# Differential attention: GpSimd takes the difference of the second head's keys, VectorE keeps the first head's and the meta columns

## The chip, the core and the metric

The kernel runs on one core of a Trainium2 chip. It has five engines with their own instruction streams, which wait for each other only through semaphores: TensorE (matrix products, into PSUM), VectorE, ScalarE, GpSimd and SyncE (which here only issues DMAs; GpSimd issues some too). In the profile they are PE (and PEld, its weight loads), DVE, ACT, POOL and SP. The metric is the device time of one execution in microseconds (us); the kernel is launched once.

## What is computed

The reference is a chain of two transformer blocks on 512 tokens of width 1024. The first block has two layers and 16 meta tokens ahead of the sequence (528 positions). Each layer mixes four branches: a windowed attention with sinks (A), an attention with rotary positions (B), a differential attention (C) and a bidirectional gated linear attention (D). The change lies in C:

```
s = einsum(q, k) * scale + bias            # per head two components, comp 0 and 1
p = softmax(s)                             # over all 528 keys
a = p[:, 0] - lam * p[:, 1]                # the difference
o = einsum(a, v)
o = rms_norm(o, sub_g) * (1 - lambda_init)
```

## The kernel before

It is written directly in instructions of each engine, so each engine does its work in the order in which its function issues it. `att` is the list of attention steps. A step of C is one tile of 128 queries (the fifth tile has the 16 meta queries; layer 1 leaves it out) and one pair of heads. Its four cells are two heads with two components each, so layer 0 has 10 such steps and layer 1 has 8.

One step runs like this. TensorE makes the scores of the four cells (L1656; L1649 makes those of the meta keys). VectorE takes the meta scores to SBUF (L3331, L3339), then adds the bias and takes the row minimum, one instruction per cell (`minima`, L3315; 512 columns, and a short one that reads the minimum out). ScalarE does the exponentials with their sums (`exps`, L2519). VectorE takes the reciprocals (L3351) and, in L3354, the factor `cfac` = -lam * sum of comp 0 / sum of comp 1 of each head, and marks them with the semaphore `att_r`. Then `difference` (L3365) computes for each of the two heads p0 = p0 + cfac * p1 in place over 528 columns, 16 meta and 512 keys, with one scalar_tensor_tensor each, and marks `att_mix`. `kept` is where in the tile `temps` the four cells of a step lie: 4 x 528 columns, two steps in turn.

TensorE then transposes the differences (`turn_probs(c, 0)` for the meta columns of both heads, L1686, and the keys of the first head, L1689; `turn_probs(c, 1)` for those of the second, L1689); ScalarE copies them out of PSUM (L2533, L2536); TensorE multiplies by the values (L1715), and L1701 spreads the reciprocals. Each iteration n of TensorE's `attention` does the scores of step n, the values of step n - 2, the first transposition of step n - 1, then a `fill_piece` (24 matrix products of another branch, L1747 to L1749) and then the second transposition of step n - 1. VectorE's iteration n does `ratios` and `difference` of step n - 1 and then the minima of step n, and at some steps `scaled` (L3389) and a subtraction that splits weights (L2951).

GpSimd has no part in C before. Ahead of the attention of layer 0 it issues the first five of 24 sets of DMAs (`layer_step`, through `block_sums`, L1333 and L1335), which add up weights of layer 1 in DRAM; each set waits (`sums_moved`) until the one before has landed. In layer 1 it issues the last of these sets and three of another chain (`last_step`). It then waits for `rope`, its part of the rotary stage (L1198, L1216, L1219, L1223), which stands in the attention A that follows C. `head_roots`, `head_stats`, `head_ratios` and `head_spread` belong to the norms of C's and D's heads, later in each layer.

Of the kernel before, what the change touches and what calls it, by code (L numbers as in the profile page):

```python
# [278 lines left out]
def build(nc, ins, out_dram):  # L279
    with ExitStack() as ctx:  # L280
# [213 lines left out]
        def level_product(eng, e, src, rows, lev, upper):  # L494
# [29 lines left out]
        names += """att_scores att_meta att_min att_es att_exp att_esink  # L524
            att_r att_mix att_turned att_pt att_ptm att_pv att_spread att_out y_ready
            c_squared c_stat c_stat_ready c_rooted c_spread c_ready""".split()

        names += """sums_rounded log_high log_low gate_floored dz_gate dz_log state_cleared g_sums g_exp g_kf g_query_x g_key_x g_z g_ez
            g_kz g_pairs g_masked g_at g_half g_o g_state g_unit state_ready o_squared o_stat o_stat_ready o_rooted
            o_spread o_scaled dmix_ready""".split()  # L530

# [581 lines left out]
        def stat_blocks(kind, l):  # L1113

            return [(P, 0, 16), (META, 16, 20)][:1 if kind == "c" and l else 2]

        def planes(rows):

            return 1 + (NLEV - 1 if rows == P else 4)
# [27 lines left out]
        def _(pool):  # L1147
# [116 lines left out]
            def head_roots(kind, l):  # L1264

                for i, (rows, a, z) in enumerate(stat_blocks(kind, l)):
                    ap = ostat[0:rows, a:z]
                    pool.wait_ge(S[kind + "_stat_ready"], 2 * l + i + 1)
                    nc.gpsimd.tensor_tensor(ap, ap, neghalf[0:rows, :].to_broadcast([rows, z - a]), ALU.pow
                                            ).then_inc(S[kind + "_rooted"], 1)  # L1270

# [43 lines left out]
            def block_sums(step, wp, n):  # L1315
# [3 lines left out]
                for q in range(NSUMS):  # L1319
# [11 lines left out]
                    for out, x, plus in moves:  # L1331
# [5 lines left out]
                        moved_sums[0] += 16  # L1337

            for ly in layers:
                l = ly["l"]  # L1340
                if l:
                    full(pool, layers[l - 1]["ffn"]["down"][1][-1])
                    pool.wait_ge(S["ada_summed"], MODS // 2)
                    load_biases()
                for step in range(19, 24) if l else range(5):
                    layer_step(step)
                for step in range(3) if l else ():
                    last_step(step)
                rope(ly)
                for step in () if l else range(5, 9):  # L1350
                    layer_step(step)
                for step in range(3, 6) if l else ():
                    last_step(step)
                first_gate_lows(ly)
                head_roots("c", l)
                key_factors(ly)
                head_roots("o", l)
                residual_back(l)
                if l == 0:
                    ada_stream()  # L1360
                    residual_out(ly["ffn"]["ready"])
            else:
                second_block()
# [4 lines left out]
        def _(pe):  # L1368
# [293 lines left out]
            def turn_probs(c, j):  # L1662
                n, rows = c["n"], c["rows"]
                if c["kind"] == "C":
                    pe.wait_ge(S["att_mix"], c["mixed0"] + 2)
                else:
                    pe.wait_ge(S["att_exp"], c["cell0"] + (2 if c["metas"] else j + 1))
# [146 lines left out]
            def head_stats(kind, l, sq, tiles):  # L1814

                pe.wait_ge(S[kind + "_squared"], 2 * (l + 1))
                for t, (a, z) in tiles:
                    for hp in range(2):
                        last = mm(PS[0:z - a, 5, 4 * t + 2 * hp:4 * t + 2 * hp + 2], sq[hp][:, a:z], headmean,
                                  start=True, stop=True, skip_group_check=True)  # L1820
                last.then_inc(S[kind + "_stat"], 1)

            def head_spread(kind, l, tiles):

                pe.wait_ge(S[kind + "_rooted"], 2 * l + len(stat_blocks(kind, l)))
                for hp in range(2):
                    flat = PS[:, 2 * hp:2 * hp + 2, :].rearrange("p a b -> p (a b)")
                    for t, (a, z) in tiles:
                        for c0, c1 in [(a, z)] if z <= 512 else [(a, 512), (512, z)]:
                            for i in range(2):  # L1830
                                h = 4 * t + 2 * hp + i
                                last = mm(flat[64 * i:64 * i + 64, c0:c1], ostat[0:z - a, h:h + 1].to_broadcast([z - a, HD]),
                                          ident[0:z - a, c0 - a:c1 - a], start=True, stop=True, skip_group_check=True)
                last.then_inc(S[kind + "_spread"], 1)

# [1042 lines left out]
        def _(dve):  # L2878
# [480 lines left out]
            def difference(c):  # L3359
# [3 lines left out]
                for j in range(2):  # L3363
                    p0, p1 = (SB[0:rows, c["kept"] + 2 * j + comp, :] for comp in range(2))
                    V.scalar_tensor_tensor(out=p0, in0=p1, scalar=cfac[0:rows, 2 * (n % 4) + j:2 * (n % 4) + j + 1],  # L3365
                                           in1=p0, op0=ALU.mult, op1=ALU.add).then_inc(S["att_mix"], 1)
# [92 lines left out]
            def head_ratios(kind, l):  # L3459

                dve.wait_ge(S[kind + "_stat"], l + 1)
                for rows, a, z in stat_blocks(kind, l):
                    V.tensor_scalar(ostat[0:rows, a:z], PS[0:rows, 5, a:z], EPS, None, ALU.add
                                    ).then_inc(S[kind + "_stat_ready"], 1)

# [45 lines left out]
            def linear_attention(ly):  # L3511
# [67 lines left out]
                merge(ly, 1)  # L3579
                dve.wait_ge(S["c_spread"], l + 1)  # L3580
                c0 = META * l
# [34 lines left out]
                merge(ly, made[0] + 2)  # L3616
                dve.wait_ge(S["o_spread"], l + 1)
                dve.wait_ge(S["o_scaled"], 2 * (l + 1))
# [440 lines left out]
```

## Time and profile before

| | |
|---|---|
| time, median of 3 runs | 2983.24 us (2982.55 to 2983.50) |
| the profiled execution | 2986.24 us, its span 2984.4 us |
| TensorE busy | 2930.9 us, 98% |
| VectorE, ScalarE, GpSimd busy | 1909.2, 1138.4, 377.6 us |
| C in layer 0 | from about 99 to 172 us |
| C in layer 1 | from about 1152 to 1211 us |
| mean granted clock of TensorE | 0.993 |

Busy time of TensorE is modelled and is not its peak. "Idle before" in brackets is how long an engine had waited ahead of an instruction, and for whom. A VectorE instruction is recorded from its issue, and the next one is issued some 0.08 us before it ends. "x2" joins two instructions in a row.

### The profile page before, as it was taken

To read this page: it belongs to the slowest core of one execution; us is meant where nothing else is said; L and a number is where in the kernel's file an instruction comes from. 1 tells how busy PE (TensorE), PEld (TensorE's weight loads), DVE (VectorE), ACT (ScalarE), POOL (GpSimd) and SP (SyncE) were. 2 spreads that over 40 slices of the span, in tenths; PEclk is the share of its full clock that TensorE was granted. 3 is DMA by queue.
4 is the path that set the end of the run, shared out by engine and by line. 5 is a ranking of instruction groups with operands and counts; after the bars stand their busy time and mean duration, and the time that the engine had idled before them with its cause. 6 is when DMAs were issued, how large, how long until landed. Compare 5 with 4: busy or idle time off the path is not lost.

```text
span 2984.4 us, 57272 instructions
## 1 busy us (share of the span) xinstructions
PE 2930.9 (98%) x23772; PEld 2627.7 (88%) x23772; DVE 1909.2 (64%) x3760; ACT 1138.4 (38%) x2030; POOL 377.6 (13%) x610
## 2 busy tenths in 40 slices
PE   9999999999999999999999999999999999999998
PEld 8777999999999998789999899987888886799997
DVE  5574677557777756647765767677636555685565
ACT  4655223232212235552323434344222232664353
POOL 0242433000000020324320000001100000000000
PEclk9999999999999999999999999999999999999999
DMA  6725766234555574347533444438723331134452
GB/s 205 211 57 139 187 147 164 72 142 157 196 192 170 193 212 132 75 122 188 145 117 114 156 142 161 156 125 210 190 89 134 139 128 43 58 115 156 143 174 91
DMA packets 119513, 428.69 MB, mean 144 GB/s; under 512 B 14248, under 2 KB 16680, under 8 KB 114264
## 3 DMA queue, kind: packets, MB, share of 16 engines
q1 hardware_dynamic: 67032, 261.52, 25.5%
q0 software_dynamic: 52224, 163.51, 20.8%
q8 instruction: 190, 3.11, 0.4%
q14 instruction: 67, 0.55, 0.1%
HBM read 414.35 MB, written 109.01 MB: 175 GB/s over the span
## 4 chain that ended last, share of the span: by engine, by line
PE 88%; DVE 5%; ACT 4%; issue 2%; DMA 1%; POOL 1%; SPq 0%; DVEq 0%; ACTq 0%; POOLq 0%
PE acc L1385 14%; PE acc L1386 13%; PE acc L1387 13%; PE acc L1847 5%; PE acc L1848 5%; PE acc L1849 5%; PE acc L2113 4%; PE acc L2114 4%; PE acc L2115 4%; ACT temps L2519 2%; PE acc L1715 2%; PE acc L1656 1%; PE acc L1420 1%; PE acc L2131 1%; PE acc L1892 1%
## 5 line engine op out<-in xcount | busy, mean ns | idle before, releaser
L2255 ACT ACTIVATE toep_r<-ring 128x1024 fp32r<-128x1024 f32 (+2 forms) x216 | 251.4, 1165 | 322.4 <-PE acc L1387 322.3
L1386 PE MATMUL acc<-normed_r,toep_r 128*128 128x264 f32 (+2 forms) x1120 | 356.9, 319 | 0.0
L2951 DVE TENSOR_TENSOR ring_r<-ring,toep_r 128x1024 fp32r<-128x1024 f32 (+2 forms) x212 | 287.6, 1358 | 95.3 <-ACT toep_r L2255 94.7
L1387 PE MATMUL acc<-work_r,ring_r 128*128 128x264 f32 (+2 forms) x984 | 323.7, 329 | 0.0
L1847 PE MATMUL acc<-residual_r,toep_r 128*128 128x264 f32 (+1 forms) x1024 | 302.2, 295 | 1.6 <-DVE mixed L3389 1.6
L1848 PE MATMUL acc<-normed_r,toep_r 128*128 128x264 f32 (+1 forms) x1024 | 293.8, 287 | 0.0
L1849 PE MATMUL acc<-residual_r,ring_r 128*128 128x264 f32 (+1 forms) x1024 | 292.4, 286 | 0.0
L1385 PE MATMUL acc<-work_r,toep_r 128*128 128x264 f32 (+2 forms) x828 | 268.6, 324 | 0.7 <-DVE ring_r L2961 0.6
L1386 PE MATMUL acc<-work_r,toep_r 128*128 128x264 f32 (+2 forms) x720 | 231.4, 321 | 0.0
L1386 PEld LDWEIGHTS acc<-normed_r,toep_r 128*128 128x128 f32 x1120 | 210.5, 188 | 14.5
L1847 PEld LDWEIGHTS acc<-residual_r,toep_r 128*128 128x128 f32 x1024 | 196.8, 192 | 8.0 <-DVE mixed L3389 1.9
L1385 PE MATMUL acc<-mixed_r,toep_r 128*128 128x264 f32 x704 | 202.9, 288 | 0.0
L1387 PEld LDWEIGHTS acc<-work_r,ring_r 128*128 128x128 f32 x984 | 185.1, 188 | 17.3
L1387 PE MATMUL acc<-mixed_r,ring_r 128*128 128x264 f32 x704 | 199.4, 283 | 0.0
L2665 ACT ACTIVATE toep<-acc 128x264 f32<-128x264 f32 (+1 forms) x128 | 49.7, 388 | 389.6 <-PE acc L1849 389.6
L1848 PEld LDWEIGHTS acc<-normed_r,toep_r 128*128 128x128 f32 x1024 | 197.0, 192 | 1.4
L1849 PEld LDWEIGHTS acc<-residual_r,ring_r 128*128 128x128 f32 x1024 | 197.7, 193 | 0.0
L1385 PEld LDWEIGHTS acc<-work_r,toep_r 128*128 128x128 f32 x828 | 155.6, 188 | 15.2 <-issue 1.5
L1385 PE MATMUL acc<-temps_r,toep_r 128*128 128x512 f32 (+1 forms) x416 | 157.0, 377 | 0.3 <-DVE ring_r L2951 0.3
L1387 PE MATMUL acc<-temps_r,ring_r 128*128 128x512 f32 (+1 forms) x416 | 155.4, 374 | 0.0
L2519 ACT ACTIVATE temps<-temps,small 128x528 f32<-128x528 f32 (+6 forms) x176 | 113.3, 644 | 92.0 <-DVE small L3315 91.8
L1386 PEld LDWEIGHTS acc<-work_r,toep_r 128*128 128x128 f32 x720 | 135.4, 188 | 10.5
(618 smaller groups left out, 8121.7 us busy)
## 6 DMA issues: line engine op xcount, KB each, us to landing
ring<-in_w_pair SPq DMA_DIRECT2D x120, 512.0 KB, 4.0
sums_store<-in_w_pair POOLq DMA_DIRECT2D x80, 512.0 KB, 8.9
ring<-in_w_gb SPq DMA_DIRECT2D x64, 640.0 KB, 4.5
ring<-in_w_down SPq DMA_DIRECT2D x32, 704.0 KB, 4.2
lower_store<-in_w_pair POOLq DMA_DIRECT2D x20, 1024.0 KB, 10.4
sums_store<-sums_store POOLq DMA_DIRECT2D x40, 512.0 KB, 5.2
extra<-in_w_ada POOLq DMA_DIRECT2D x18, 1024.0 KB, 7.3
toep<-in_w_ada POOLq DMA_DIRECT2D x18, 1024.0 KB, 6.4
```

The lines of the kernel that those rows point to most:

```text
L1385: mm(out, wh, xh[:, a:z], start=i == 0, stop=False)
L1386: mm(out, wh, xl[:, a:z], start=False, stop=False)
L1387: last = mm(out, wl, xh[:, a:z], start=False, stop=end)
L1847: mm(out, wh, xh[:, a:z], start=m == 0, stop=False)
L1848: mm(out, wh, xl[:, a:z], start=False, stop=False)
L1849: last = mm(out, wl, xh[:, a:z], start=False, stop=m == len(xs) - 1)
L2113: mm(out, wh, xh, start=begins and k == 0, stop=False, skip_group_check=True)
L2114: mm(out, wh, xl, start=False, stop=False, skip_group_check=True)
L2115: last = mm(out, wl, xh, start=False, stop=k == 3, skip_group_check=True)
L2255: A(high(ld), slot(ld), ACT.Copy).then_inc(S["w_high"], 1)
L2519: A(x, x, ACT.Exp, bias=negm[0:rows, i:i + 1], scale=-1.0, accum_out=sums[0:rows, i:i + 1]).then_inc(S["att_exp"], 1)
L2951: V.tensor_tensor(low(ld), slot(ld), high(ld), ALU.subtract).then_inc(S["w_low"], 1)
```

## The change

The difference of the second head is split by columns. VectorE keeps the first head over all 528 columns and takes the 16 meta columns of the second. GpSimd takes the second head's 512 key columns, in two operations: p1 = p1 * cfac, then p0 = p0 + p1, and marks a new semaphore `att_mix_keys`, for which TensorE's second transposition now waits in place of `att_mix`. GpSimd waits for `att_r` itself. In layer 0 its sets 1 to 4 of DMAs move between these pairs (after steps 0, 2, 4 and 6 of C). To free semaphores for the new one, those of the head norms of C and D are joined into `heads_...`, whose counts run over both; an unused one of C goes too.

```
@@ gpsimd
+            def key_differences(c):
+
+                n, rows = c["n"], c["rows"]
+                pool.wait_ge(S["att_r"], n + 1)
+                p0, p1 = (SB[0:rows, c["kept"] + 2 + comp, META:L] for comp in range(2))
+                factor = cfac[0:rows, 2 * (n % 4) + 1:2 * (n % 4) + 2].to_broadcast([rows, SEQ])
+                link(nc.gpsimd.tensor_tensor(p1, p1, factor, ALU.mult))
+                nc.gpsimd.tensor_tensor(p0, p0, p1, ALU.add).then_inc(S["att_mix_keys"], 1)
...
-                for step in range(19, 24) if l else range(5):
+                for step in range(19, 24) if l else range(1):
                     layer_step(step)
                 for step in range(3) if l else ():
                     last_step(step)
+                for n in range(*ly["C"]):
+                    key_differences(att[n])
+                    if l == 0 and (n - ly["C"][0]) % 2 == 0 and n - ly["C"][0] < 8:
+                        layer_step(1 + (n - ly["C"][0]) // 2)
                 rope(ly)
@@ tensor: turn_probs
-                    pe.wait_ge(S["att_mix"], c["mixed0"] + 2)
+                    pe.wait_ge(*((S["att_mix_keys"], c["mixed0"] // 2 + 1) if j else (S["att_mix"], c["mixed0"] + 2)))
@@ vector: difference
-                    p0, p1 = (SB[0:rows, c["kept"] + 2 * j + comp, :] for comp in range(2))
+                    p0, p1 = (SB[0:rows, c["kept"] + 2 * j + comp, 0:META if j else L] for comp in range(2))
@@ head norms, in all four functions alike
-                pe.wait_ge(S[kind + "_rooted"], 2 * l + len(stat_blocks(kind, l)))
+                pe.wait_ge(S["heads_rooted"], blocks_before(kind, l) + len(stat_blocks(kind, l)))
```

On VectorE, at the first step of C in layer 0, this stands before (small is where `cfac` lies, acc is PSUM, toep the bias, ISA the minimum instructions of L3315):

```order
L3351 RECIPROCAL small<-small 128x4 [waits att_exp]
L3354 SCALAR_TENSOR_TENSOR small<-small 128x2 [waits vector_chain]
L3365 SCALAR_TENSOR_TENSOR temps<-temps,small 128x528 [waits att_r]
L3365 SCALAR_TENSOR_TENSOR temps<-temps,small 128x528
L3331 SCALAR_TENSOR_TENSOR temps<-acc,toep 128x2x16 [waits att_scores]
L3331 SCALAR_TENSOR_TENSOR temps<-acc,toep 128x2x16
```

and this of the change (its lines are 17 further down: L3382 is `difference`):

```order
L3368 RECIPROCAL small<-small 128x4 [waits att_exp]
L3371 SCALAR_TENSOR_TENSOR small<-small 128x2 [waits vector_chain]
L3382 SCALAR_TENSOR_TENSOR temps<-temps,small 128x528 [waits att_r]
L3382 SCALAR_TENSOR_TENSOR temps<-temps,small 128x16
L3348 SCALAR_TENSOR_TENSOR temps<-acc,toep 128x2x16 [waits att_scores]
L3348 SCALAR_TENSOR_TENSOR temps<-acc,toep 128x2x16
```

Nothing has changed its place; the second difference has 16 columns in place of 528.

On GpSimd, from the first set of DMAs in layer 0, before:

```order
L1335 DMA lower_store<-in_w_pair 128x2x1024
L1333 DMA sums_store<-in_w_pair 128x2x512 [waits sums_moved]
L1333 DMA lower_store<-in_w_pair 128x2x512
L1335 DMA sums_store<-sums_store 128x2x512 [waits sums_moved]
L1335 DMA sums_store<-in_w_pair 128x2x512
```

and of the change (L1349 and L1350 are the pair, L1337 and L1339 the DMAs; the ISA row is GpSimd's own, ahead of its first arithmetic):

```order
L1339 DMA lower_store<-in_w_pair 128x2x1024
L1349 ISA
L1349 TENSOR_TENSOR temps<-temps,small 128x512 [waits att_r]
L1350 TENSOR_TENSOR temps<-temps 128x512 [waits pool_chain]
L1337 DMA sums_store<-in_w_pair 128x2x512 [waits sums_moved]
L1337 DMA lower_store<-in_w_pair 128x2x512
L1349 TENSOR_TENSOR temps<-temps,small 128x512 [waits att_r]
L1350 TENSOR_TENSOR temps<-temps 128x512 [waits pool_chain]
L1349 TENSOR_TENSOR temps<-temps,small 128x512 [waits att_r]
L1350 TENSOR_TENSOR temps<-temps 128x512 [waits pool_chain]
L1339 DMA sums_store<-sums_store 128x2x512 [waits sums_moved]
```

The DMAs that stood one behind the other are now parted by waits for VectorE's factors, and the pairs behind them stand behind their waits for landed moves.

## Rows read from the trace of the kernel before

**Rows 1.** The page's part 4, the chain that ended last, by engine.
```profile
PE 88%; DVE 5%; ACT 4%; issue 2%; DMA 1%; POOL 1%; SPq 0%; DVEq 0%; ACTq 0%; POOLq 0%
```

**Rows 2.** The chain of waits in layer 0: start us, us, what.
```profile
112.82 0.59 DVE temps L3365
...
115.55 2.27 ACT temps L2519 x6
```

**Rows 3.** The waits of 99 to 172 us: in total, times, longest.
```profile
ACT temps L2519 <- DVE small L3315: 25.1, 11, 3.1
...
PE acc L1686 <- DVE temps L3331: 2.0, 2, 1.2
```

**Rows 4.** Line L3365: duration ns min/median/max, first and last start, forms.
```profile
L3365 DVE SCALAR_TENSOR_TENSOR temps<-temps,small x36: 749/762/769, 105.9 to 1209.6; 128x528 f32<-128x528 f32 x32, 16x528 f32<-16x528 f32 x4
```

**Rows 5.** Timeline of VectorE, layer 0: start us, us, engine line op.
```profile
105.61 0.22 DVE L3354 SCALAR_TENSOR_TENSOR small<-small 128x2 f32<-128x2 f32 x1
105.87 1.45 DVE L3365 SCALAR_TENSOR_TENSOR temps<-temps,small 128x528 f32<-128x528 f32 x2
...
106.55 0.76 DVE L3365 SCALAR_TENSOR_TENSOR temps<-temps,small 128x528 f32<-128x528 f32 x1
107.23 0.28 DVE L3331 SCALAR_TENSOR_TENSOR temps<-acc,toep 128x32 f32<-128x32 f32 x2
...
107.80 0.75 DVE L3315 CUSTOM_DVE_ANT_0 temps<-acc,toep,small 128x512 f32<-128x512 f32 x1
```

**Rows 6.** Timeline of VectorE and TensorE at the stage's end in layer 1.
```profile
1208.96 1.45 DVE L3365 SCALAR_TENSOR_TENSOR temps<-temps,small 128x528 f32<-128x528 f32 x2
...
1210.69 0.39 PE L1686 MATMUL acc<-con,temps 128*16 128x128 f32 x2
```

**Rows 7.** Timeline of GpSimd, and its groups by form (busy us, mean ns).
```profile
180.94 1.02 POOL L1219 TENSOR_TENSOR work<-work,con 128x384 f32<-128x384 f32 x1
...
L1262 POOL TENSOR_TENSOR ring_r<-ring,toep_r 128x1280 fp32r<-128x1280 f32 x4 | 11.6, 2904 | 48.2 <-ACT toep_r L2255 48.2
```

**Rows 8.** Timeline of VectorE and GpSimd in the rotary stage.
```profile
180.92 0.62 DVE L3315 CUSTOM_DVE_ANT_0 temps<-acc,toep,small 128x400 f32<-128x400 f32 x1
...
181.47 0.51 DVE L3350 TENSOR_TENSOR small<-small 128x2 f32<-128x2 f32 x1
...
192.97 1.21 DVE L2951 TENSOR_TENSOR ring_r<-ring,toep_r 128x1024 fp32r<-128x1024 f32 x1
192.99 2.10 POOL L1219 TENSOR_TENSOR work<-work,con 128x384 f32<-128x384 f32 x1
```

**Rows 9.** Timeline of VectorE and GpSimd in the linear attention.
```profile
317.14 0.23 DVE L503 TENSOR_TENSOR work<-work 128x64 f32<-128x64 f32 x1
317.18 0.39 POOL L503 TENSOR_TENSOR work<-work 128x64 f32<-128x64 f32 x1 [1.08 <-ACT work L2684]
...
317.28 0.38 DVE L503 TENSOR_TENSOR work<-work 128x64 f32<-128x64 f32 x1
```

**Rows 10.** Timeline of VectorE and GpSimd, start of the rotary stage.
```profile
173.86 2.35 DVE L2951 TENSOR_TENSOR ring_r<-ring,toep_r 128x1024 fp32r<-128x1024 f32 x2
174.10 2.19 POOL L1198 TENSOR_TENSOR small<-small 128x6 f32<-128x6 f32 x1 [31.29 <-DVE small L3285]
```

**Rows 11.** Timeline of GpSimd: its idle time before, in brackets.
```profile
103.39 1.20 POOL L1333 DMA_DIRECT2D sums_store<-in_w_pair  x1 [7.40 <-DMA lower_store<-in_w_pair]
...
227.49 1.43 POOL L1335 DMA_DIRECT2D sums_store<-sums_store  x2 [14.30 <-DMA lower_store<-in_w_pair]
...
1213.32 2.25 POOL L1198 TENSOR_TENSOR small<-small 128x6 f32<-128x6 f32 x1 [63.60 <-DVE small L3285]
```

**Rows 12.** Timeline of VectorE and TensorE at the stage's end in layer 0.
```profile
169.69 1.44 DVE L3365 SCALAR_TENSOR_TENSOR temps<-temps,small 16x528 f32<-16x528 f32 x2
...
171.18 0.20 PE L1686 MATMUL acc<-con,temps 16*16 16x16 f32 x2 [0.49 <-DVE temps L3365]
...
173.10 0.35 PE L1689 MATMUL acc<-con,temps 16*128 16x16 f32 x3
```

More of the change, by code:

```diff
@@ L524, in build @@
         names += """att_scores att_meta att_min att_es att_exp att_esink
-            att_r att_mix att_turned att_pt att_ptm att_pv att_spread att_out y_ready
-            c_squared c_stat c_stat_ready c_rooted c_spread c_ready""".split()
+            att_r att_mix att_mix_keys att_turned att_pt att_ptm att_pv att_spread att_out y_ready
+            c_squared c_ready""".split()
         names += """sums_rounded log_high log_low gate_floored dz_gate dz_log state_cleared g_sums g_exp g_kf g_query_x g_key_x g_z g_ez
-            g_kz g_pairs g_masked g_at g_half g_o g_state g_unit state_ready o_squared o_stat o_stat_ready o_rooted
-            o_spread o_scaled dmix_ready""".split()
+            g_kz g_pairs g_masked g_at g_half g_o g_state g_unit state_ready o_squared heads_stat heads_stat_ready heads_rooted
+            heads_spread o_scaled dmix_ready""".split()
         names += """u_shifted proj_full proj_read dt_ready ssm_args ssm_tanh ssm_sin fc_ready ba_ready b_turned bt_staged ssm_made
@@ L1115, in stat_blocks, with blocks_before @@
             return [(P, 0, 16), (META, 16, 20)][:1 if kind == "c" and l else 2]
+        def blocks_before(kind, l):
+            return 4 * l + (len(stat_blocks("c", l)) if kind == "o" else 0)
         def planes(rows):
@@ L1267, in head_roots @@
                     ap = ostat[0:rows, a:z]
-                    pool.wait_ge(S[kind + "_stat_ready"], 2 * l + i + 1)
+                    pool.wait_ge(S["heads_stat_ready"], blocks_before(kind, l) + i + 1)
                     nc.gpsimd.tensor_tensor(ap, ap, neghalf[0:rows, :].to_broadcast([rows, z - a]), ALU.pow
-                                            ).then_inc(S[kind + "_rooted"], 1)
+                                            ).then_inc(S["heads_rooted"], 1)
             def residual_out(ready):
@@ L1820, in head_stats @@
                                   start=True, stop=True, skip_group_check=True)
-                last.then_inc(S[kind + "_stat"], 1)
+                last.then_inc(S["heads_stat"], 1)
             def head_spread(kind, l, tiles):
-                pe.wait_ge(S[kind + "_rooted"], 2 * l + len(stat_blocks(kind, l)))
+                pe.wait_ge(S["heads_rooted"], blocks_before(kind, l) + len(stat_blocks(kind, l)))
                 for hp in range(2):
@@ L1833, in head_spread @@
                                           ident[0:z - a, c0 - a:c1 - a], start=True, stop=True, skip_group_check=True)
-                last.then_inc(S[kind + "_spread"], 1)
+                last.then_inc(S["heads_spread"], 1)
             def gate_piece(ly, q):
@@ L3459, in head_ratios @@
             def head_ratios(kind, l):
-                dve.wait_ge(S[kind + "_stat"], l + 1)
+                dve.wait_ge(S["heads_stat"], 2 * l + "co".index(kind) + 1)
                 for rows, a, z in stat_blocks(kind, l):
                     V.tensor_scalar(ostat[0:rows, a:z], PS[0:rows, 5, a:z], EPS, None, ALU.add
-                                    ).then_inc(S[kind + "_stat_ready"], 1)
+                                    ).then_inc(S["heads_stat_ready"], 1)
             def forget_gates(l, w):
@@ L3579, in linear_attention @@
                 merge(ly, 1)
-                dve.wait_ge(S["c_spread"], l + 1)
+                dve.wait_ge(S["heads_spread"], 2 * l + 1)
                 c0 = META * l
@@ L3616, in linear_attention @@
                 merge(ly, made[0] + 2)
-                dve.wait_ge(S["o_spread"], l + 1)
+                dve.wait_ge(S["heads_spread"], 2 * l + 2)
                 dve.wait_ge(S["o_scaled"], 2 * (l + 1))
```

## The prediction

> **What bounds the kernel now.** I read the page first: TensorE carries 88% of the chain that ended last [rows 1]. So only what delays TensorE, or lets it run where it now waits, can move the time. The change lies in the differential attention (C) of both layers, so I read the chain of waits there next. One of its steps (one query tile, one pair of heads) is a loop between VectorE and ScalarE: the difference at 112.82, then the minima, the exponentials from 115.55 [rows 2], and then the next reciprocal and difference. From the difference at 105.87 [rows 5] to that at 112.82 it is 6.95 us. ScalarE waits for VectorE 11 times in this stage, 25.1 us in all, while TensorE waits for VectorE's writes for only 2.0 us [rows 3]: the loop and TensorE's own work are nearly even, and the loop is a little the longer. Every 0.1 us more on VectorE between the end of one set of exponentials and the start of the next is paid by TensorE; 0.1 us less is worth something only while TensorE still waits.
>
> **The change part by part.** There are 36 differences [rows 4], two per step: 10 steps in layer 0 (five query tiles) and 8 in layer 1 (four).
>
> What VectorE loses. The first difference starts at 105.87, the second is issued at 106.55, and what follows them (L3331) at 107.23 [rows 5]: 1.36 us for two, 0.68 each. The second shrinks from 528 to 16 columns. By the 0.28 us of the two L3331 operations on 32 columns [rows 5] it should be issued and out of the way in about 0.1 us. Taken alone that is 0.58 us less per step.
>
> What GpSimd gains. Per step a multiply and an add of 128x512. No row has that form. A 128x384 multiply took 1.02 us with nothing in its way and the 128x1280 subtraction 2.90 us [rows 7]; on the line between them 512 columns take 1.29 us. As one ends about 0.1 us before the next begins, the pair ends 2.7 us after it may begin.
>
> How the two meet. Both engines wait for the same mark, the factor made by L3354. VectorE's L3354 ends at 105.83 and its next instruction starts 0.04 us later [rows 5]; where both wait for one mark of ScalarE, GpSimd starts 0.04 us behind VectorE [rows 9]. So VectorE's first difference should go first and GpSimd's multiply asks while it runs. The trace shows what then happens when both read two operands from SBUF: they take turns. At 192.97 VectorE's L2951 began, 0.02 us ahead of a GpSimd multiply that takes 1.02 us alone; the multiply took 2.10 us, so it waited for VectorE to be through. In the other order, a VectorE operation on two columns issued at 181.47 took 0.51 us, to 181.98, within 0.02 us of the end (181.96) of GpSimd's multiply begun at 180.94 [rows 7, 8]. The nearest picture of the new code is the linear attention: VectorE begins a 64-column product at 317.14, GpSimd at 317.18, VectorE issues its second at 317.28. The first took 0.23 us, the second 0.38 us: GpSimd got in between [rows 9]. The distance of 0.04 us at the start is that of the changed kernel.
>
> So I take: first difference 0.68 us, then GpSimd's multiply 1.29 us, and only then the 16-column difference, which like the two-column one ends with it. VectorE's next instruction starts 0.68 + 1.29 = 1.97 us after the first instead of 1.36: 0.61 us **more** per step, for an operation that needed 0.1 us. The ends for this unknown are 0.58 us less (not held at all) and 1.95 us more (third rival). I take the value next to the row with the same order of starts.
>
> The add comes after that. The VectorE instructions then due (L3331, L3339, L3315) read PSUM or one operand; L3315 took 0.62 us for 400 columns beside a GpSimd multiply [rows 8] and 0.75 for 512 with GpSimd idle [rows 5], the same per column, so the add should cost VectorE nothing.
>
> The Trainium skill, page "SBUF — State Buffer", section "Who interferes with whom", says that a VectorE instruction with two SBUF inputs contends with a GpSimd instruction that reads SBUF, and that the one that comes first holds the shared pair for its whole length. That names scalar_tensor_tensor too, of which no row here shows a meeting with GpSimd: by it the 0.61 us stand, without it the 0.58 us less. The trace agrees for the plain products; it does not for one pair: GpSimd's power of 6 columns waited at 174.10 behind the first of two VectorE subtractions and ended in 2.19 us, yet the two took 2.35 us together, as long as undisturbed [rows 10]. It computes long and reads little, so the port was held for its reading only.
>
> The sum. Layer 0: 10 steps x 0.61 = 6.1 us. After the last of them TensorE already waits 0.49 us for the differences [rows 12], so all of it arrives. Layer 1: 8 x 0.61 = 4.9 us, but there TensorE reaches L1686 at 1210.69, and the last differences end at 1208.96 + 1.45 = 1210.41 [rows 6], so 0.28 us of slack is used up first: 4.6 us. Together 10.7 us.
>
> The new wait of TensorE (the second transposition waits for GpSimd) I cost at nothing. GpSimd's pair ends 0.68 + 1.29 + 0.1 + 1.29 = 3.4 us after the first difference starts. The tightest place is the end of the stage in layer 0: difference at 169.69, transposition at 173.10 [rows 12], which itself moves on by the 0.6 us of its last step; elsewhere a fill of 24 products lies between and the distance is over 5 us. Queued behind that wait are the scores of a later step, so if the cover went, each us would be paid in full.
>
> GpSimd's DMAs. In layer 0 four sets of moves now stand between the pairs and wait for the set before. Before, GpSimd waited 7.40 us for one at 103.39 and 14.30 us at 227.49 [rows 11]. Two steps last 15 us, so a pair will be held up for a us or two at most, within the cover above. The moves come later than before by 6 us (the first: after the pair that begins at 105.9) to some 16 us (the fourth), and nothing reads them until the next layer's feed-forward. In layer 1 GpSimd idles 63.6 us up to the rotary stage [rows 11]: nothing in the way. The joined semaphores of the head statistics only rename waits: nothing.
>
> The profiled execution took 2986.24 us, 1.8 us of them outside the span; the median of the runs is 2983.24, 3.0 us less. The sum, made against the profiled one, gives 2996.9, and against the median **2993.9 us**. After these stages I give 0.2 us back for slack that TensorE has in the first attention steps that follow: 2993.7 us. That is 0.35% slower, beyond the 0.2% (6.0 us) that a measurement of this kernel can tell from no change.
>
> **The rivals.** First: the 16-column difference is not held. For it speaks the power of 6 columns [rows 10] and that no row shows this form of instruction meeting GpSimd. Then the loop is 0.58 us shorter per step, but TensorE's own work soon ends last: what it can take back is two waits, of 2.0 us together [rows 3], by 0.58 us each, as much again in layer 1 by the same pattern, and the 0.49 us at the end of layer 0 [rows 12]: 1.2 + 1.2 + 0.5 = 2.9 us, and perhaps 0.6 more in short gaps. I take 3.5: 2979.7 us, no change that can be told.
>
> Second, on the far side: GpSimd asks first. Then each step holds multiply 1.29, first difference 0.68, the add (it asks 0.1 us after the multiply and is next in turn) 1.29 and the last difference: 3.3 us in place of 1.36, 1.95 us more. 18 steps less the slack make 34.8 us: 3018 us. It decides if GpSimd sees the mark sooner than VectorE sees its own; against it is that it came 0.04 us later than VectorE in rows 9. By the rule of the same page and section, that the order of issue decides and not the form, this would be the outcome of a lead of GpSimd of any size.
>
> Third: the meetings are partial. GpSimd's multiply holds VectorE for only part of its length (its reading runs ahead of its writing), or a wait for moves puts some multiplies past the differences, so that half of the steps lose and half gain: 18 steps x 0 = 2983 to 2988 us.
>
> **How the numbers follow.** Forecast 0.67, first rival 0.16, second 0.06, third 0.11. Around the forecast the size of the hold moves it by 0.15 us per step: 2991 to 2997. The range that holds 8 in 10 takes the forecast with its own spread, the third rival and most of the first: 2979.5 to 2998. Faster by over 0.2% (under 2977.3) only if the first rival frees more than the waits seen: 0.04. Within 0.2% are the first and the third rival and a low end of the forecast: 0.25. Slower by more: 0.71.
>
> **What would show it.** In the changed kernel's profile: the 16-column difference lasts 1.2 to 1.4 us, its end within 0.05 us of the end of GpSimd's multiply; first difference to L3331's successor is 1.97 us; the steps of layer 0 last 7.5 us and more; GpSimd's 512-column multiply lasts near 2.0 us as recorded (it includes the wait), its add 1.3 us; TensorE's wait before L1686's successor returns in nearly every step; no wait of TensorE for GpSimd's add. The forecast is wrong if the 16-column difference takes 0.1 us (first rival), or if the 528-column one takes about 2 us (second).

## The result, and the profile after

The changed kernel is slower, and by more than forecast. Its median is 3010.06 us (6 runs, 3001.28 to 3011.98) against 2983.37 us for the kernel before (6 runs); the ratio is 1.0087, interval 1.0077 to 1.0098: about 26 us by the ratio. The forecast of 2993.7 us (2979.5 to 2998) had the direction and missed the size. The profiled execution took 3008.26 us, its span 3006.4 us, 22.0 us longer than that of before.

The chain that ended last is split by engine as before [rows 1], with TensorE still at 88%:

```profile
PE 88%; DVE 5%; ACT 4%; issue 2%; DMA 1%; POOL 0%; SPq 0%; DVEq 0%; ACTq 0%; POOLq 0%
```

In what follows the line numbers are those of the changed kernel, where those named here stand 17 further down than before (the difference L3365 is L3382, L3331 is L3348, L1686 is L1703). GpSimd's multiply is L1349, its add L1350. First the form of the new operations: for one line each, the durations in ns (least, median, most), the first and the last start, and the forms.

```profile
L3382 DVE SCALAR_TENSOR_TENSOR temps<-temps,small x36: 767/1233/1650, 105.9 to 1233.0; 128x528 f32<-128x528 f32 x16, 128x16 f32<-128x16 f32 x16, 16x528 f32<-16x528 f32 x2, 16x16 f32<-16x16 f32 x2
```

```profile
L1349 POOL TENSOR_TENSOR temps<-temps,small x18: 1029/1039/1614, 105.9 to 1231.4; 128x512 f32<-128x512 f32 x16, 16x512 f32<-16x512 f32 x2
```

```profile
L1350 POOL TENSOR_TENSOR temps<-temps x18: 1273/1606/1617, 107.6 to 1232.5; 128x512 f32<-128x512 f32 x16, 16x512 f32<-16x512 f32 x2
```

VectorE's 36 differences took 749 to 769 ns each before [rows 4]. Now their median is 1233 and their longest 1650. And the multiply's median is 1039, next to its least: in most steps it waits for nobody. It goes first. The timeline shows two kinds of step. The first is like the forecast (VectorE and GpSimd at the first step of layer 0; start, duration, line, operation):

```profile
105.86 1.70 DVE L3382 SCALAR_TENSOR_TENSOR temps<-temps,small 128x528 f32<-128x528 f32 x2
105.91 1.61 POOL L1349 TENSOR_TENSOR temps<-temps,small 128x512 f32<-128x512 f32 x1 [11.18 <-DVE small L3371]
107.48 0.27 DVE L3348 SCALAR_TENSOR_TENSOR temps<-acc,toep 128x32 f32<-128x32 f32 x2
107.60 1.28 POOL L1350 TENSOR_TENSOR temps<-temps 128x512 f32<-128x512 f32 x1
```

VectorE's 528-column difference goes first, GpSimd's multiply is recorded as 1.61 us because it waits, and VectorE's next instruction (L3348) starts 1.62 us after the first difference, 0.26 us later than the 1.36 us of before [rows 5]. The other kind:

```profile
120.28 2.81 DVE L3382 SCALAR_TENSOR_TENSOR temps<-temps,small 128x528 f32<-128x528 f32 x2
120.32 1.04 POOL L1349 TENSOR_TENSOR temps<-temps,small 128x512 f32<-128x512 f32 x1 [4.24 <-DVE small L3371]
...
121.44 1.61 POOL L1350 TENSOR_TENSOR temps<-temps 128x512 f32<-128x512 f32 x1
...
123.01 0.28 DVE L3348 SCALAR_TENSOR_TENSOR temps<-acc,toep 128x32 f32<-128x32 f32 x2
```

Here the multiply takes its own 1.04 us, although it starts 0.04 us **behind** VectorE. VectorE's 528-column difference waits for it, the add waits for that difference (1.61 us recorded), and VectorE's 16-column difference waits for the add. L3348 starts 2.73 us after the first difference: 1.37 us later than before. Over both layers 3 steps are of the first kind and 15 of the second: 3 x 0.26 + 15 x 1.37 = 21.3 us more in VectorE's loop.

TensorE pays nearly all of it. The waits in the stage of layer 0, here 99 to 182 us (in total, times, longest), to be held against rows 3:

```profile
ACT temps L2536 <- DVE small L3332: 33.7, 10, 3.8
...
PE acc L1703 <- DVE temps L3348: 8.4, 8, 1.4
```

ScalarE waits 33.7 us for VectorE in place of 25.1, and TensorE's products wait 8.4 us in eight waits where it had two of 2.0 us together [rows 3]. At the end of layer 1, where I had counted on slack [rows 6], TensorE now waits 1.06 us:

```profile
1231.38 2.80 DVE L3382 SCALAR_TENSOR_TENSOR temps<-temps,small 128x528 f32<-128x528 f32 x2
...
1234.24 0.39 PE L1703 MATMUL acc<-con,temps 128*16 128x128 f32 x2 [1.06 <-DVE temps L3382]
```

No wait of any engine for the add (L1350) shows in the trace. At the stage's end something else joins in. TensorE and VectorE, last step of layer 0, to be held against rows 12:

```profile
178.58 2.79 DVE L3382 SCALAR_TENSOR_TENSOR temps<-temps,small 16x528 f32<-16x528 f32 x2
178.63 1.03 POOL L1349 TENSOR_TENSOR temps<-temps,small 16x512 f32<-16x512 f32 x1 [5.24 <-DVE small L3371]
...
181.43 0.22 PE L1703 MATMUL acc<-con,temps 16*16 16x16 f32 x2 [1.99 <-DVE temps L3382]
...
182.00 3.01 PE L1489 MATMUL acc<-con 128*128 128x264 f32 x6
...
185.47 1.65 PE L1673 MATMUL acc<-work 64*128 64x16 f32 x8
```

TensorE waited 1.99 us where it had waited 0.49 [rows 12], and right behind it six products of 264 columns take 3.01 us (1.60 before), and the eight of 16 columns 1.65 us (0.93 before). The granted clock says why. Stretches of the changed kernel (the stretch and its length, busy us of PE, PEld, DVE, ACT and POOL with their instructions, then the granted clock as a share of 2.4 GHz, the share of the DMA engines, GB/s):

```profile
172.00:178.00 6.00, 5.13 (x56) 3.93 (x54) 5.00 (x14) 3.33 (x11) 1.39 (x1) 1.00 0.00 0
178.00:182.00 4.00, 1.87 (x30) 1.33 (x28) 3.75 (x9) 2.37 (x6) 2.63 (x2) 0.86 0.80 266
182.00:195.00 13.00, 13.00 (x77) 10.88 (x76) 8.73 (x29) 3.54 (x16) 5.03 (x5) 0.52 0.00 0
196.00:205.00 9.00, 8.33 (x82) 6.43 (x80) 5.67 (x20) 5.49 (x16) 5.54 (x6) 1.00 0.01 2
```

From 182 to 195 us TensorE ran at 0.52, that is nearly all the time at its lower level of 1.2 GHz. The fall lies in the stretch from 178 to 182 us, in which it was busy for 1.87 of 4 us. Before, the work from the end of this stage to 190 us ran at 1.00. Pairing the n-th instruction of TensorE in one trace with the n-th in the other shows how the delay grows (start before: delay after, us):

```
  98.1:  0.0      start of the stage, layer 0
 139.9: +3.0      (2 steps of 5 of the long kind so far)
 171.6: +10.4     end of the stage
 180.7: +15.4     behind it, at the lower clock
 504.9: +15.4
 562.1: +11.9     a stretch at the lower clock that only the kernel before had here
1145.1: +12.0     start of the stage, layer 1
1218.4: +23.6     end of the stage (all 8 steps long; two short stretches at the lower clock)
1324.0: +22.2
2967.4: +22.0
```

In all, the lower level was granted for 34.1 us before and 41.0 us after within these two executions (left out are the last 6.1 us of either span, at the lower level too, in which TensorE has no work), which costs at most half of it: 17.1 and 20.5 us. So of the 22.0 us, 3.4 are the clock's by this count and 18.6 the waits' (21.3 in the steps, 2.7 of them slack). One execution says little on the clock, though. Over all runs the mean granted clock is 0.9920 for the changed kernel (6 runs) and 0.9954 for the kernel before (34 runs, those beside experiments 1 to 4); times their spans that is 24.1 and 13.8 us lost. By that count about 15 us of the loss are waits and about 10 the clock. The single values have three digits, so each is good to some 1.5 us, their means to less. Why the waits are 15 us by this count and 18.6 in the two traces I can't say; a part may be that a lower clock costs nothing while TensorE waits.

### The profile page after: what moved, and what is told of

It is laid out like the page before. It is cut to its first block, busy times and chain, and to the rows that moved or that the text cites. A ratio compares the mean times of both kernels' runs of the same rounds, so it can differ in the third digit from the quotient of the medians.

```text
span 3006.4 us, 57308 instructions
## 1 busy us (share of the span) xinstructions
PE 2935.2 (98%) x23772; PEld 2629.9 (87%) x23772; DVE 1929.4 (64%) x3760; ACT 1137.9 (38%) x2030; POOL 424.6 (14%) x646
## 4 chain that ended last, share of the span: by engine, by line
PE 88%; DVE 5%; ACT 4%; issue 2%; DMA 1%; POOL 0%; SPq 0%; DVEq 0%; ACTq 0%; POOLq 0%
PE acc L1402 13%; PE acc L1403 13%; PE acc L1404 13%; PE acc L1864 5%; PE acc L1865 5%; PE acc L1866 5%; PE acc L2130 4%; PE acc L2131 4%; PE acc L2132 4%; ACT temps L2536 2%; PE acc L1732 2%; PE acc L1673 1%; PE acc L1437 1%; PE acc L2148 1%; PE acc L1909 1%
```

## The experiments

There are nine experiments: eight other kernels, and the changed one again. "Port" is short for what VectorE and GpSimd take turns at when both read two operands from SBUF, as the prediction has it. Each experiment ran beside the kernel before, with these medians: 2983.02 us for experiments 1 to 4 (34 runs), 2982.58 for 5 to 7 (15), 2983.42 for 8 and 9 (15), against 2983.37 for the changed kernel's first runs (6). The ratios are to these. Of the other kernels there are 5 runs (experiments 7 and 9), 6 (the changed one), 10 to 12 (1 to 5 and 8), and one of experiment 6. "First" is the number of the 18 steps in which GpSimd takes the port ahead of VectorE's first difference, "next" the distance from the start of that first operation to VectorE's next instruction after the differences, "clock" the mean granted clock over all runs. "First" and "next" are from one trace each.

```
kernel                    median us  ratio [interval]         clock   first  next us
before                    2983.02    1                        0.9954    -    1.36
changed                   3010.06    1.0087 [1.0077, 1.0098]  0.9920   15    2.73 (1.62)
1 GpSimd waits for both   2977.11    0.9984 [0.9975, 0.9993]  0.9952    0    0.83
2 GpSimd 0.15 us later    2988.41    1.0015 [1.0007, 1.0024]  0.9949    0    1.62
3 small difference first  2991.68    1.0026 [1.0015, 1.0036]  0.9942   16    1.72
4 moves only              2982.41    0.9999 [0.9990, 1.0008]  0.9954    -    1.36
5 no add                  2989.18    1.0019 [1.0010, 1.0028]  0.9954   15    1.72
6 plain products          3021.39    one run                  0.989     0    3.24
7 VectorE longer          3008.72    1.0084 [1.0070, 1.0098]  0.9928    -    2.66
8 GpSimd waits for first  2976.43    0.9980 [0.9971, 0.9988]  0.9957    0    0.83
9 changed, again          3002.05    1.0065 [1.0051, 1.0079]  0.9940   14    2.73 (1.62)
```

**1. GpSimd waits for VectorE's differences.** (This is also the better version.)

```
-                pool.wait_ge(S["att_r"], n + 1)
+                pool.wait_ge(S["att_mix"], c["mixed0"] + 2)
```

> GpSimd's multiply waits until both differences of VectorE are done, instead of asking with them. Theory (port order): in the changed kernel GpSimd's multiply goes ahead of VectorE's 528-column difference in 15 of 18 steps, and the add ahead of the 16-column one, so VectorE's next instruction starts 2.73 us after the first in place of 1.36. Here nothing stands in VectorE's way: next instruction near 0.8 us after the first, and the time falls to 2976 to 2984 us, about or a little under the kernel before, TensorE being the bound again. First rival (TensorE waits for the keys of the second head that GpSimd makes late): the pair begins 0.8 us later and ends near 3.1 us after the first difference starts, later than the 2.77 us of now, so the time stays at 3010 us or rises. Second rival (the moved sets of GpSimd's DMAs): stays near 3010 us.

Measured: 2977.11 us, 5.9 us under the kernel before, at the same mean clock. VectorE and GpSimd in the second step of layer 0:

```profile
112.94 0.91 DVE L3382 SCALAR_TENSOR_TENSOR temps<-temps,small 128x528 f32<-128x528 f32 x2
...
113.77 0.28 DVE L3348 SCALAR_TENSOR_TENSOR temps<-acc,toep 128x32 f32<-128x32 f32 x2
113.94 1.03 POOL L1349 TENSOR_TENSOR temps<-temps,small 128x512 f32<-128x512 f32 x1 [1.67 <-DVE temps L3382]
...
115.05 1.30 POOL L1350 TENSOR_TENSOR temps<-temps 128x512 f32<-128x512 f32 x1
```

Both differences together last 0.91 us, and the next instruction starts 0.83 us after the first. That is so in 8 of the 18 steps; in the others it starts 0.87 to 1.18 us after it. In the seventh step, for one, TensorE's scores (L1673) end at 147.62 us and L3348, which reads them, starts at 147.74: there TensorE is the slower of the two again. GpSimd's pair ends at 116.35, 3.41 us after the first difference starts, later than in the changed kernel (2.77 us, and 3.02 in its short steps). Had TensorE's wait for the keys been the cause, this would have been the slowest of all. In its trace TensorE waits for the add once, 0.3 us, with a weight load. Both rivals of this expectation fall, since the moved DMAs are all there too.

**2. GpSimd asks a little later.**

```
                 pool.wait_ge(S["att_r"], n + 1)
+                link(nc.gpsimd.memset(late, 0.0))
```

(`late` is one more column in SBUF, which nothing reads.)

> As the changed kernel, but GpSimd writes one spare column (a memset of 128x1) between the mark and its multiply, so that it asks some 0.1 us later. Theory (port order): VectorE's 528-column difference then always comes first; all 18 steps look like the 3 short ones of now (next instruction of VectorE 1.62 us after the first, 0.26 us more than before): 18 x 0.26 = 4.7 us less about 1 us of slack, and no or less low clock: 2985 to 2990 us. First rival (late keys for TensorE): the pair ends later than now, 3010 us or more. Second rival (moved DMAs): 3010 us. A third, that it is not the moment of asking that decides who goes first: the two orders stay mixed, 3003 to 3010 us.

Measured: 2988.41 us, as the theory had it. One more small operation on GpSimd makes the changed kernel 14 to 22 us faster (3002.05 and 3010.06 us on its two occasions, neither of them beside this experiment). Its lines stand 2 further down than the changed kernel's:

```profile
120.03 1.70 DVE L3384 SCALAR_TENSOR_TENSOR temps<-temps,small 128x528 f32<-128x528 f32 x2
120.06 0.10 POOL L1348 MEMSET small<- 128x1 f32 x1 [4.22 <-DVE small L3373]
...
120.23 1.46 POOL L1351 TENSOR_TENSOR temps<-temps,small 128x512 f32<-128x512 f32 x1
...
121.65 0.28 DVE L3350 SCALAR_TENSOR_TENSOR temps<-acc,toep 128x32 f32<-128x32 f32 x2
```

The multiply starts 0.20 us behind VectorE in place of 0.04 and is recorded with 1.46 us: it waited. In all 18 steps the next instruction of VectorE starts 1.62 us after the first difference. This is the order of the forecast, and its true price: 18 x 0.26 = 4.7 us, measured 5.4.

**3. The 16-column difference first.**

```
-                for j in range(2):
+                for j in (1, 0):
```

> As the changed kernel, but VectorE makes the 16-column difference first and the 528-column one second. Theory (port order, turns of whole operations): whoever wins the start, VectorE's 528-column difference waits for one multiply (1.04 us) and not for the add, which asks only after it: 0.06 + 1.0 + 0.69 = 1.8 us to VectorE's next instruction in place of 2.73, 0.45 us more than before per step. 18 x 0.45 = 8.1 us less 1 us of slack, plus up to 3 us of lower clock: 2990 to 2994 us. Rival (GpSimd keeps the port for both of its operations): 16-column difference, multiply, add, difference, near 3 us: 3010 us or more.

Measured: 2991.68 us. The next instruction starts at 1.72 us in 16 steps and at 1.63 in two: 16 x 0.36 + 2 x 0.27 = 6.3 us more; the other 2.4 of the 8.7 us are within what the clock took (17.4 us lost against 13.8). GpSimd keeps the port for one operation, not for both. I had taken 0.45 us per step; that is 0.1 too much.

**4. The moves alone.** No pair on GpSimd, VectorE makes all differences, DMAs and semaphores as changed:

```
-                    key_differences(att[n])
...
-                    p0, p1 = (SB[0:rows, c["kept"] + 2 * j + comp, 0:META if j else L] for comp in range(2))
+                    p0, p1 = (SB[0:rows, c["kept"] + 2 * j + comp, :] for comp in range(2))
...
-                    pe.wait_ge(*((S["att_mix_keys"], c["mixed0"] // 2 + 1) if j else (S["att_mix"], c["mixed0"] + 2)))
+                    pe.wait_ge(S["att_mix"], c["mixed0"] + 2)
```

> The changed kernel without its pairs on GpSimd: VectorE makes all 36 differences of 528 columns, TensorE waits for VectorE alone, and only the joined semaphores and the four sets of DMAs stay in their new place in the program of GpSimd. Theory (port order): the kernel before, 2981 to 2986 us. Rival (the moved sets of DMAs, or the semaphores, carry a part of the loss): up to 3010 us.

Measured: 2982.41 us, ratio 0.9999 (0.9990 to 1.0008). The DMAs' new place and the joined semaphores cost nothing that this can tell.

**5. No add.**

```
-                link(nc.gpsimd.tensor_tensor(p1, p1, factor, ALU.mult))
-                nc.gpsimd.tensor_tensor(p0, p0, p1, ALU.add).then_inc(S["att_mix_keys"], 1)
+                nc.gpsimd.tensor_tensor(p1, p1, factor, ALU.mult).then_inc(S["att_mix_keys"], 1)
```

> The changed kernel without GpSimd's add (so the keys' difference of the second head is left out; GpSimd only multiplies). Theory (port order): where GpSimd goes first, VectorE's 528-column difference waits 0.88 us for the multiply as now, but the 16-column one follows it at once, so VectorE's next instruction starts at 1.57 + 0.1 = 1.7 us in place of 2.73: 0.35 us more than before per step, 18 x 0.35 = 6.3 us less 1 us of slack, plus 0 to 3 us of lower clock: 2987 to 2992 us. It says that the add carries about 1.0 of the 1.37 us that a step loses. Rival (the multiply is what costs, or GpSimd beside VectorE slows it whatever it does): 3000 us or more.

Measured: 2989.18 us, 6.6 us over the kernel before. GpSimd still goes first in 15 steps:

```profile
120.49 1.79 DVE L3381 SCALAR_TENSOR_TENSOR temps<-temps,small 128x528 f32<-128x528 f32 x2
120.53 1.04 POOL L1349 TENSOR_TENSOR temps<-temps,small 128x512 f32<-128x512 f32 x1 [5.59 <-DVE small L3370]
...
122.21 0.27 DVE L3347 SCALAR_TENSOR_TENSOR temps<-acc,toep 128x32 f32<-128x32 f32 x2
```

The next instruction starts 1.72 us after the first difference. So with the multiply alone ahead a step is 0.36 us longer than before, and the add ahead of the 16-column difference makes the other 1.01 of the 1.37. The 0.36 is net: with nothing ahead the next instruction would start at 0.83 us (experiment 1), so the wait for the multiply is 0.89 us, of which the shorter second difference had saved 0.53. Of the 1.90 us of waiting in a long step, an operation of 16 columns that waits for one of 512 carries a little over half.

**6. Plain products on VectorE.** This asks why GpSimd wins although it starts second.

```
+                    if j == 0:
+                        link(V.tensor_tensor(p1, p1, cfac[0:rows, 2 * (n % 4):2 * (n % 4) + 1].to_broadcast([rows, L]), ALU.mult))
+                        V.tensor_tensor(p0, p0, p1, ALU.add).then_inc(S["att_mix"], 1)
+                        continue
```

> VectorE makes the first head's difference as two plain TENSOR_TENSOR operations (a product with the factor broadcast, then a sum) in place of one SCALAR_TENSOR_TENSOR; everything else as changed. In the trace of the changed kernel GpSimd starts 44 to 57 ns after VectorE; it goes first in all meetings up to 50 ns and VectorE in those of 51 and 57 ns (one of 51 ns apart), while the plain products of the linear attention keep the lead at 44 ns. Theory A (the form decides: a SCALAR_TENSOR_TENSOR with its scalar in SBUF asks for the port some 50 ns after its start, a plain TENSOR_TENSOR at once): VectorE's product takes its own 0.6 to 0.75 us first in all 18 steps, and GpSimd's multiply is recorded with 1.6 us or more. Theory B (only the two engines' delay to the mark decides, whatever the form): GpSimd goes first in about 15 of 18 steps, and VectorE's product is recorded with 1.6 us. The time tells nothing between them: both ways each step holds two products and two sums in turns, and about 3.5 us go by before VectorE's next instruction; 3015 to 3030 us.

Measured: 3021.39 us in one run. VectorE's product is L3383 here:

```profile
L3383 DVE TENSOR_TENSOR temps<-temps,small x18: 696/708/709, 105.8 to 1245.5; 128x528 f32<-128x528 f32 x16, 16x528 f32<-16x528 f32 x2
```

```profile
L1349 POOL TENSOR_TENSOR temps<-temps,small x18: 1548/1560/1563, 105.8 to 1245.5; 128x512 f32<-128x512 f32 x16, 16x512 f32<-16x512 f32 x2
```

All 18 products of VectorE took 696 to 709 ns, none waited; all 18 multiplies of GpSimd took 1548 ns or more, all waited. They start 0.04 to 0.06 us behind VectorE, as in the changed kernel. Of theory A this much holds: at this distance what VectorE issues decides who goes first, and not the distance. That the asking comes some 50 ns after the start is not shown. The product also takes its factor as an operand rather than as a scalar, so which of the two (form or scalar) delays the asking isn't told apart.

**7. VectorE longer, GpSimd idle.** From experiment 4:

```
+                both = SB[0:rows, c["kept"]:c["kept"] + 2, :]
+                link(V.scalar_tensor_tensor(out=both, in0=both, scalar=1.0, in1=both, op0=ALU.mult, op1=ALU.max))
```

> No work for GpSimd: VectorE makes all differences of 528 columns (as before), and ahead of each pair one more operation of 1056 columns that changes nothing (each value times 1, the larger of it and itself), about 1.45 us with its own wait, near the 1.37 us of a step in which GpSimd goes first. 18 x 1.45 = 26.1 us, less the 2.5 us of slack that the changed kernel showed (21.2 us in its steps, 18.6 us in its span but for the clock) = 23.6 us. Theory (the loss goes by VectorE's loop alone, and the lower clock follows from TensorE's longer waits): like the changed kernel it loses more than the steps do, by 3 to 10 us of lower clock: 3009 to 3017 us, mean granted clock under 0.994. Rival (the extra beyond the steps comes from GpSimd being at work beside TensorE, not from its waits): 3006 to 3008 us at a granted clock of 0.995 to 0.996, as before.

Measured: 3008.72 us. The added operation with its wait took 1.30 us, not 1.45: 18 x 1.30 = 23.4 us, less the slack of 2.7 gives 20.7, and 26.1 were measured. In the place of the stage's end in layer 0 the clock falls here too:

```profile
181.00:187.50 6.50, 4.45 (x46) 3.38 (x44) 6.22 (x18) 3.80 (x12) 0.41 (x1) 0.87 0.44 159
188.00:194.00 6.00, 6.00 (x55) 5.43 (x52) 4.70 (x18) 1.83 (x7) 1.84 (x2) 0.61 0.00 0
```

The mean clock is 0.9928 (21.7 us lost against 13.3 in the kernel before beside it). GpSimd has no pair in these steps, and the loss is that of the changed kernel, with its share of lower clock. The time lies between the two ranges, 0.3 us under the theory's and 0.7 over the rival's. The clock tells them apart: it is under the theory's 0.994, and the rival had it at 0.995 to 0.996. So the rival, that the extra comes from GpSimd at work, falls.

**8. GpSimd waits for the first difference only.**

```
-                pool.wait_ge(S["att_mix"], c["mixed0"] + 2)
+                pool.wait_ge(S["att_mix"], c["mixed0"] + 1)
```

> As the first experiment (GpSimd waits for VectorE's differences), but GpSimd waits for the first of the two only, that of 528 columns. Theory (port order, asking times): that mark comes when the first difference has ended, 0.77 us after its start, and by then VectorE has issued the 16-column one (at 0.69) and it has the port: GpSimd starts near 0.8 instead of 1.0 us, VectorE's next instruction still at 0.83: 2974 to 2981 us, no difference from the first experiment. Rival (GpSimd gets between the two differences): the 16-column one is held about 1 us, VectorE's next instruction near 1.8 us: 2988 us or more.

Measured: 2976.43 us, the same as experiment 1 (their intervals overlap), with the multiply 0.84 to 0.86 us behind the first difference and VectorE's next instruction at 0.83 where nothing else holds it. A lead of about 0.16 us for the 16-column difference is enough in all 18 steps.

**9. The changed kernel again**, with no edit, on the chip of experiment 8.

> The changed kernel once more, beside the kernel before on the chip of the other experiments. Theory (port order): 3006 to 3012 us; in its trace the number of steps in which GpSimd goes first may differ from 15 of 18, since the two engines ask within some 10 ns of a tie, but it stays over half; mean granted clock 0.991 to 0.994. If the loss were of one chip or one session: back towards 2983 us.

Measured: 3002.05 us, 4 us under what I expected. 14 steps are of the long kind (15 in the first trace), and which ones they are differs: the fourth step was short and is long, the sixth and eighth were long and are short. The mean clock is 0.9940 (18.0 us lost, 24.1 in the first runs). The mean of span times clock is 2983.0 us here and 2982.9 in the first runs, so what differs between the two occasions is the clock and not the waits. For the kernel before it is 2967.8 and 2968.7: the waits cost 14 to 15 us on both, and the clock 5 to 10.

## Why the prediction was wrong

**What bounds the kernel**: right. The loop of VectorE and ScalarE in the differential attention carries the change, and all but 2.7 us of the time added there reaches TensorE. Experiment 7 shows it without GpSimd.

**"So VectorE's first difference should go first and GpSimd's multiply asks while it runs"**: this is the step that failed. The distance of 0.04 us was forecast rightly, but not what it means. I took it from plain products [rows 8, 9], where the engine that starts first by the record has the port; the differences are of another form. In 15 of 18 steps GpSimd had it (14 in the repeat), and in experiment 6, with plain products on VectorE, in none. The Trainium skill, page "SBUF — State Buffer", section "Who interferes with whom", says that issue order and not the form of the operation decides who blocks. (It covers this form by its two inputs in SBUF; that it names it, as the working has it, is wrong.) This trace differs: by the starts in the record VectorE came first every time, and a plain product in its place (its factor an operand) turned 15 of 18 into none. What that section says of the whole operation being waited for holds: the 528-column difference lasts 1.65 us where it waits for a multiply of 1.04, and the 16-column one ends 0.03 us behind the add's end.

**The price of each order** was too high in both. The multiply takes 1.03 to 1.04 us, not 1.29: my line through two sizes came from operations with two full operands or other strides, this one has a broadcast factor. The add, with two full operands, does take the 1.29 us (1.28 to 1.32). The multiply's shorter time is 0.25 of the 0.35 us that 1.97 was too much. The other 0.10: a multiply that has waited ends 0.90 us after the first difference does, not 1.04 plus a start, and the next instruction starts 0.05 us before the multiply's end. In the forecast's order the next instruction comes at 1.62 us (experiment 2), not at 1.97, and the kernel at 2988.4 us; in the second rival's order at 2.73, not at 3.3. The two errors hid each other: too much for an order that mostly didn't come, and the range's upper end of 2998 us left out the one that did. (The 1.95 us for the order in which GpSimd asks first is the second rival's; the working calls it the third's once.) With 0.06 for the second rival I had called 0.04 us of lead safe, with no row in which a difference of this form met GpSimd.

**"The add should cost VectorE nothing"**: wrong in the order that came. It goes ahead of the 16-column difference and costs 1.01 us a step (experiment 5). In the other order it is right: after L3348 the instructions keep their durations.

**TensorE's new wait at nothing**: right, even with the pair ending at 3.41 us (experiment 1). **The DMA sets**: right, and cheaper than "a us or two": no multiply of the 18 starts more than 0.06 us after VectorE's difference, and experiment 4 is at 0.9999. **Slack**: 0.28 us forecast, 2.7 found in the two traces.

**The clock** isn't in the sum at all. I read it as 1.00 in this stage and took it as given; with TensorE waiting about 1 us in most steps, and 2 us at the end, it was granted its lower level more often, 5 to 10 us in a mean run. The trace of before had two falls that follow a stretch in which TensorE waited: it was busy for 3.64 us of 280 to 285 us and for 3.01 us of 1308 to 1312, and from 286 to 295 and from 1313 to 1319 it had 0.50. But it fell behind full work too (busy for 5.00 us of 546 to 551, and at the lower level from 551.4), so no row tells beforehand when it would fall. That longer waits bring it about is what experiments 2, 3, 7 and the changed kernel together speak for (mean clock 0.9949, 0.9942, 0.9928, 0.9920 to 0.9940 for 0.26, 0.36, 1.30 and mostly 1.37 us a step, against 0.9954). Experiment 5 stands out: 0.36 us a step too, and 0.9954. Only for the long steps, of experiment 7 and the changed kernel, is the effect beyond doubt. And a fall at the end of this stage takes no long steps: short ones (3.4 us) show there in the traces of experiments 2, 3 and 8 too, and one of 10.2 us in that of experiment 5; what the long steps add is more and longer ones.

**The gain that the change could have had** is that of the first rival: 5.9 us in experiment 1, where I had estimated 3.5. It took one other mark to wait for.

## What to carry to other kernels

When VectorE and GpSimd are released by the same mark and both read two operands from SBUF, which of them goes first can hang on some 10 ns and on the form of the operation, and the other then waits for a whole operation: chain the side that is off the critical path behind the other's mark. Beware of the short operation behind a long one: taking 512 of 528 columns from VectorE left it an operation of 16 columns that waited longer than the whole had taken. And read the granted clock of the work that follows a new wait, not only the wait.

## What the runs showed of the hardware

- A SCALAR_TENSOR_TENSOR on VectorE with its scalar in SBUF, started 0.04 to 0.06 us ahead of a GpSimd multiply, mostly loses the port to it (15, 14, 16 and 15 of 18 steps in the changed kernel, its repeat and experiments 3 and 5). At a recorded lead of 43 to 45 ns GpSimd had it 48 times of 48; the 12 that VectorE won are among the 24 with 50 to 57 ns. A plain TENSOR_TENSOR with a lead of 45 to 57 ns kept it 18 times of 18 (experiment 6), and with 0.2 us of lead the first form kept it 18 times of 18 too (experiment 2).
- GpSimd's multiply of 128x512 fp32 by a broadcast column takes 1.03 to 1.04 us, its add of two such operands 1.28 to 1.32 us (experiment 1, where the port is free for the multiply).
- The clock's lower level comes and goes between executions of one kernel: 2977.4 to 2989.6 us for the kernel before, with a mean clock of 0.998 to 0.994 beside it. The 5.9 us between experiment 1 and the kernel before rest on 12 and 34 runs.
